# The products with V in an attention loop: the small and the large pair of query blocks in one run, two runs per head in place of four

## The chip, the cores and the metric

The kernel runs on one core of a Trainium2 chip. The metric is the device time of one execution in microseconds (us). It is compared with the kernel before, whose median over 3 runs is 2402.06 us.

## The reference, cut to what matters

Two decoder layers over 1024 tokens of width 1024. Each layer has a mixer (attention with 8 heads beside a causal convolution with 31 taps, then an output projection) and a gated feed-forward part. All is float32, and the large products are done as three products of rounded parts. Only the attention is touched here:

```
for window, dilation in DILATED_PATTERNS:
    o_i, lse_i = _dilated_branch(qp, kp, vp, window, dilation)   # softmax(q k^T * dh**-0.5 + band) v
...
w = jax.nn.softmax(jnp.stack(lses, axis=0), axis=0)
o = jnp.einsum('gbsh,gbshd->bshd', w, jnp.stack(outs, axis=0).astype(jnp.float32))
```

The kernel computes the mixture as one causal softmax: the logarithm of the number of patterns in which a key counts is added to its score (tile logcount), so for a query block of 128 rows all key blocks up to its own are needed.

## The kernel before, in words

The program is written by hand, one instruction queue for each engine, with semaphores between them. What stands in a queue is done in that order; nothing is scheduled by a tool.

Attention of a layer is a loop over steps n = 0 to 75, the same loop in the queues of TensorE (PE), ScalarE (ACT) and VectorE (DVE). There are 64 steps with work of their own: 8 heads times 8 query blocks. Within a head the blocks come in the order BLOCKS = (0, 6, 1, 7, 2, 4, 3, 5); a block b needs b + 1 key blocks. I call the steps of a head its step 0 to step 7. For each of them these things are done, each by its own engine:

- **scores** (PE, `scores`, line 597): q times k, into one of two PSUM tiles mm. It waits until DVE has read that tile two steps before.
- **mask** (DVE, `add_mask`, line 1326): adds logcount, takes the row's maximum, writes the scores to one of four tiles sc. DVE also does some taps of the convolution in these steps (line 1196).
- **exponential** (ACT, `exps`, line 931): in place in sc.
- **turn** (PE, `turn`, line 624), three steps later: transposes the key blocks of sc, up to four into each of three PSUM banks that are used in turn. A bank waits until its last content has been read.
- **copy** (ACT, `read_turn`, line 945): bank to SBUF, into pT_small (it is laid over the tile cos and bears that name in the profile) for steps 0, 2, 4, 6 and into pT_large for steps 1, 3, 5, 7. ACT does in step n of the loop first the copies of step n - 3, and then the exponential of step n.
- **products with V** (PE, `attend`, line 643): two query blocks at a time make a pair. Pair 0 is blocks 0 and 1 (steps 0 and 2) with 3 products, pair 3 is blocks 6 and 7 (steps 1 and 3) with 15, pair 1 is blocks 2 and 3 (steps 4 and 6) with 7, pair 2 is blocks 4 and 5 (steps 5 and 7) with 11. The two blocks of a pair write the two halves of the partitions, so each product uses 64 columns of the array where all other products use 128; the trace has two records for one such product. Before its first product `attend` waits for the copies of its second block, all of them.

After the four pairs ACT moves the head's result out (line 954), PE turns it back four steps later (tile sin, line 624), DVE divides by the row sums (lines 1344 and 1346), and every second head PE turns the finished heads once more (tile rinv), and ACT (line 948) and DVE (line 1336) write x_hi and x_lo. Odd heads from head 3 on have two of these last turns in their steps 1 and 3.

Where the pairs stand is in one table: ATTENDS has for each pair its step in the loop (n = 8 h + that number for head h), the pair and the step that it waits for.

Of the kernel before, what the change touches and what calls it, by code (L numbers as in the profile page):

```python
# [76 lines left out]
O_AT = 25  # L77
H_AT = 15
BLOCKS = (0, 6, 1, 7, 2, 4, 3, 5)
ATTENDS = ((6, 0, 2), (8, 3, 3), (10, 1, 6), (12, 2, 7))  # L80
LAST_STEP = STEPS + 12
DOWN = GROUPS * KT
X_UPD = 2 * KT + DOWN
# [94 lines left out]
def trunk(nc, xT, positions, weights, gains, qk_gains, conv_par, ffn_par, inv_freq, mask, outT):  # L178
    ctx = ExitStack()
    with ctx:  # L180
# [143 lines left out]
        def at(l, per_layer, base, step=0, i=0):  # L324

            return l * per_layer + i * step + base
# [16 lines left out]
        def pT(n):  # L343

            buf, qb = (pT_small, pT_large)[n % 2], BLOCKS[n % TB]
            first = qb if qb % 2 else 0
            return buf[:, first:first + qb + 1, :]
# [20 lines left out]
        def bank_read(l, f, after=0):  # L368

            return at(l, BANK_FILLS[f % TURN_BANKS], f // TURN_BANKS + 1 + after)  # L370

        def plain(eng):


            eng.sem_inc(waits_passed, 1)
# [96 lines left out]
        def _(pe):  # L472
# [15 lines left out]
            for l in range(DEPTH):  # L488
# [80 lines left out]
                def turn_v(t):  # L569

                    pe.wait_ge(mm_read, at(l, MM, U_V + t + 3))
                    if t == 0:
                        pe.wait_ge(small_read, at(l, SMALL, S_LN + 1))
                    else:
                        pe.wait_ge(v_turned, at(l, PAIRS, t))
                    src = v_raw[t]
                    for b in range(TB):
                        last = pe.transpose(stat_s[:, b * P:(b + 1) * P], src[:, b * P:(b + 1) * P], ident[:])  # L578
                    last.then_inc(v_turn_full, 1)
# [6 lines left out]
                def scores(n):  # L586
                    h, qb = n // TB, BLOCKS[n % TB]
                    b = h % 2
                    if n % TB == 0:
                        pe.wait_ge(head_loaded[b], at(l, 80 * HEADS // 2, 80 * (h // 2 + 1)))  # L590
                    pe.wait_ge(mm_read, at(l, MM, M_SCORE + n + 1))

                    keys = (qb // 2 + 1) * 2 * P
                    for a in range(0, keys, BANK):
                        z = min(a + BANK, keys)
                        for k in (k_hh, k_ll):
                            last = pe.matmul(mm[n % 2][:, a:z], q_st[b][:, qb * P:(qb + 1) * P], k[b][:, a:z],  # L597
                                             start=k is k_hh, stop=k is k_ll)
                    last.then_inc(mm_full, 1)

                def turn(f):

                    n, kind, which, a, z = FILLS[f]
                    bank = turn_bank[f % TURN_BANKS]
                    pe.wait_ge(pt_read[f % TURN_BANKS], bank_read(l, f))
                    if f == 2:

                        pe.wait_ge(v_turned, at(l, PAIRS, PAIRS))
                    if kind == "p":
                        if which == 0:  # L610

                            pe.wait_ge(statb_read, at(l, STAT_B, B_MEAN + 1))
                        pe.wait_ge(exp_done, at(l, STEPS, which + 1))
                        blocks = [sc[which % 4][:, kb * P:(kb + 1) * P] for kb in range(a, z)]
                    elif kind == "h":

                        pe.wait_ge(o_moved, at(l, HEADS, which + 1))
                        blocks = [o_turned[which % 2][:, i * P:(i + 1) * P] for i in range(4)]
                    else:

                        pe.wait_ge(o_read, at(l, HEADS, 2 * which + 4))
                        blocks = [o_nat[:, qb, :] for qb in range(a * 4, a * 4 + 4)]
                    for c, block_ in enumerate(blocks):
                        last = pe.transpose(bank[:, c * P:(c + 1) * P], block_, ident[:])  # L624
                    last.then_inc(pt_full, 1)

                def attend(h, k):

                    _, pair, second = ATTENDS[k]
                    b, hh = h // 2, h % 2  # L630
                    if h == 0 and k == 0:
                        pe.wait_ge(v_turned, at(l, PAIRS, PAIRS))
                    if k == 0 and (l or h):

                        pe.wait_ge(o_moved, at(l, HEADS, h))
                    last_fill = LAST_FILL[h * TB + second]
                    for f in range(max(0, last_fill + 1 - TURN_BANKS), last_fill + 1):
                        pe.wait_ge(pt_read[f % TURN_BANKS], bank_read(l, f, 1))
                    cols = slice(pair * P, (pair + 1) * P)
                    for kb in range(2 * pair + 2):  # L640
                        for half in range(2):
                            if kb <= 2 * pair + half:
                                last = pe.matmul(o_bank[half * HEAD_DIM:(half + 1) * HEAD_DIM, cols],  # L643
                                                 vp[b][:, kb, hh * HEAD_DIM:(hh + 1) * HEAD_DIM],
                                                 pT(h * TB + BLOCKS.index(2 * pair + half))[:, kb, :],
                                                 start=kb == 0, stop=kb == 2 * pair + half)
                    last.then_inc(step_done, 1)

                def out_part(u, b, which, k0):

                    pe.wait_ge(weights_split, at(l, UNITS, U_OUT + u + 3))
                    pe.wait_ge(mm_read, at(l, MM, M_OUT + 2 * u + b + 1))
                    for k in which:
                        cols = slice((b * 4 + k) * P, (b * 4 + k + 1) * P)
                        last = split_product(mm[b], (w_hi[u % 2][:, cols], w_lo[u % 2][:, cols]),
                                             (x_hi[:, k0 + k, :], x_lo[:, k0 + k, :]), k == 0, k == 3)
                    if k == 3:
                        last.then_inc(mm_full, 1)

                for n in range(LAST_STEP):  # L660
                    if n == STEPS + 5:
                        pe.wait_ge(o_split, at(l, 2 * PAIRS, 2 * PAIRS - 2))
                        out_part(0, 0, [0], 0)
                    if n == STEPS + 8:
                        out_part(0, 0, [1], 0)
                    if n < STEPS:
                        scores(n)
                    if n == 0:
                        turn_v(3)
                        plain(pe)  # L670
                    attends = [((n - first) // TB, k) for k, (first, _, _) in enumerate(ATTENDS)
                               if (n - first) % TB == 0 and 0 <= n - first < STEPS]
                    for h, k in attends:
                        if k % 2:
                            attend(h, k)
                    for f in range(PT):
                        if FILLS[f][0] == n and FILLS[f][1] == "p":
                            turn(f)
                    for h, k in attends:
                        if k % 2 == 0:  # L680
                            attend(h, k)
                    for f in range(PT):
                        if FILLS[f][0] == n and FILLS[f][1] in "ho":
                            turn(f)
                    if n == LAST_STEP - 1:
                        out_part(0, 0, [2], 0)
# [931 lines left out]
```

## Time and profile before

| | us |
|---|---|
| median of 3 runs (2401.87 to 2402.41) | 2402.06 |
| the profiled execution, its own time | 2402.06 |
| its span in the trace | 2400.3 |
| PE busy, share of the span | 99% |
| ACT busy, share of the span | 33% |
| DVE busy, share of the span | 64% |

The span runs from the first to the last instruction. Busy shares are averages over stages; the attention loop lies, for the first layer, between 250 and 374 us, and for the second between about 1442 and 1566 us. The TensorE clock that was granted is full speed throughout.

### The profile page before, as it was taken

The page shows a single profiled execution, that of the slowest core. Times are in us where ns is not written, and L with a number is a line of the kernel's source. Part 1 is how long each engine was busy: PE and PEld are TensorE (multiplying, and loading weights), DVE is VectorE, ACT ScalarE, POOL GpSimd, SP SyncE. Part 2 cuts the span into 40 slices and gives each one's busy share as a digit, 9 for nine tenths or more (in the row PEclk, how much of TensorE's full clock was granted, in tenths as well). Part 3 has the DMA queues.
Part 4 walks back from the last instruction along what each step waited for, and adds up shares of the span by engine and source line. Part 5 has one row for each costly group of instructions (what it writes and reads, how often), then busy time and mean ns, then how long its engine had stood idle before and what let it go on. Part 6 is the DMA issues. An engine that isn't in the chain of part 4 may idle for free.

```text
span 2400.3 us, 30716 instructions
## 1 busy us (share of the span) xinstructions
PE 2370.7 (99%) x11672; PEld 1945.4 (81%) x11672; DVE 1546.4 (64%) x1659; ACT 788.6 (33%) x1050; POOL 162.0 (7%) x57
## 2 busy tenths in 40 slices
PE   8999999999999999999999999999999999999999
PEld 6888788888888888888788887888888888888887
DVE  5999875656565555555749997755655565555555
ACT  5322675432222222222332227743322222222221
POOL 0122002100000000000102120011000000000000
PEclk9999999999999999999999999999999999999999
DMA  4323631121111111111112254301211111111111
GB/s 159 91 79 111 152 81 36 53 62 52 45 35 52 52 52 44 47 49 44 44 35 80 79 140 116 80 27 53 62 44 53 44 37 50 52 52 44 52 44 70
DMA packets 46676, 153.44 MB, mean 64 GB/s; under 512 B 7424, under 2 KB 10112, under 8 KB 46592
## 3 DMA queue, kind: packets, MB, share of 16 engines
q1 hardware_dynamic: 45728, 149.93, 21.5%
q10 hardware_dynamic: 864, 2.36, 0.2%
q8 instruction: 57, 0.93, 0.2%
q14 instruction: 27, 0.22, 0.0%
HBM read 131.02 MB, written 21.23 MB: 63 GB/s over the span
## 4 chain that ended last, share of the span: by engine, by line
PE 90%; issue 4%; DVE 4%; ACT 1%; DVEq 0%; POOLq 0%; DMA 0%; POOL 0%; SPq 0%; ACTq 0%
PE mm L485 60%; PE aux L485 20%; PE aux L643 3%; PE aux L624 3%; PE mm L597 3%; PE aux L512 1%; DVE y L1196 1%; DVE x_lo L1122 1%; PE aux L521 0%; DMA x<-xT 0%; POOLq L1504 0%; DVE sc L1326 0%; PE aux L578 0%; DVE w_lo L1110 0%; DVE o L1245 0%
## 5 line engine op out<-in xcount | busy, mean ns | idle before, releaser
L485 PE MATMUL mm<-x_hi,w_hi 128*128 128x512 f32 x1920 | 598.7, 393 | 14.3 <-DVE x_lo L1122 11.3
L485 PE MATMUL mm<-x_hi,w_lo 128*128 128x512 f32 x1920 | 594.6, 391 | 0.0
L485 PE MATMUL mm<-x_lo,w_hi 128*128 128x512 f32 x1920 | 594.1, 391 | 0.0
L485 PEld LDWEIGHTS mm<-x_hi,w_hi 128*128 128x128 f32 x1920 | 358.0, 188 | 92.0 <-issue 12.2
L485 PEld LDWEIGHTS mm<-x_lo,w_hi 128*128 128x128 f32 x1920 | 360.7, 188 | 78.3
L485 PEld LDWEIGHTS mm<-x_hi,w_lo 128*128 128x128 f32 x1920 | 360.7, 188 | 77.6
L794 ACT ACTIVATE w_hi<-w_raw 128x1024 fp32r<-128x1024 f32 x152 | 160.0, 1060 | 659.3 <-PE mm L485 461.5
L1116 DVE TENSOR_TENSOR x<-x,aux 128x1024 f32<-128x1024 f32 x176 | 214.8, 1221 | 121.2 <-PE aux L485 111.5
L1110 DVE TENSOR_TENSOR w_lo<-w_raw,w_hi 128x1024 fp32r<-128x1024 f32 x152 | 190.3, 1257 | 54.5 <-ACT w_hi L794 50.7
L1128 DVE TENSOR_TENSOR uv<-mm,rinv 128x1024 f32<-128x1024 f32 x44 | 53.9, 1225 | 220.3 <-PE mm L485 220.1
L1196 DVE SCALAR_TENSOR_TENSOR y<-u_all,cpar,y 128x512 f32<-128x512 f32 x248 | 186.9, 768 | 0.1
L1128 DVE TENSOR_TENSOR ug<-mm,rinv 128x1024 f32<-128x1024 f32 x44 | 53.9, 1225 | 181.2 <-PE mm L485 158.7
L1326 DVE CUSTOM_DVE_ANT_0 sc<-mm,logcount 128x128 f32<-128x128 f32 (+7 forms) x128 | 95.7, 755 | 46.6 <-PE mm L597 26.9
L485 PE MATMUL mm<-x_hi,q_first 128*128 128x512 f32 x384 | 121.4, 397 | 0.0
L485 PE MATMUL mm<-x_lo,q_first 128*128 128x512 f32 x384 | 121.0, 396 | 0.0
L485 PE MATMUL mm<-x_hi,k_hh_first 128*128 128x512 f32 x384 | 120.9, 396 | 0.0
L931 ACT ACTIVATE sc<-sc,small 128x128 f32<-128x128 f32 (+7 forms) x128 | 100.0, 781 | 24.2 <-DVE small L1326 23.2
L1196 DVE SCALAR_TENSOR_TENSOR y<-u_all,taps_sum,y 128x512 f32<-128x512 f32 x120 | 102.7, 855 | 2.6 <-ACT y L850 1.8
L485 PE MATMUL aux<-h_hi_odd,w_hi 128*128 128x512 f32 x320 | 101.0, 397 | 0.0
L485 PE MATMUL aux<-h_lo_odd,w_hi 128*128 128x512 f32 x320 | 100.9, 396 | 0.0
L485 PE MATMUL aux<-h_hi_odd,w_lo 128*128 128x512 f32 x320 | 100.9, 396 | 0.0
L1038 ACT ACTIVATE cg<-cg 128x1024 f32<-128x1024 f32 x44 | 46.7, 1062 | 128.5 <-DVE cg L1444 128.5
(190 smaller groups left out, 3008.0 us busy)
## 6 DMA issues: line engine op xcount, KB each, us to landing
w_raw<-weights SPq DMA_DIRECT2D x188, 512.0 KB, 3.6
qk_scratch<-m SPq DMA_DIRECT2D x64, 128.0 KB, 2.1
qk_scratch<-o SPq DMA_DIRECT2D x64, 128.0 KB, 2.1
x_hi<-qk_scratch SPq DMA_DIRECT2D x32, 256.0 KB, 6.2
q_first<-qk_scratch SPq DMA_DIRECT2D x8, 512.0 KB, 4.6
k_hh_first<-qk_scratch SPq DMA_DIRECT2D x16, 256.0 KB, 5.8
k_ll_first<-qk_scratch SPq DMA_DIRECT2D x16, 256.0 KB, 6.5
x_hi<-qk_scratch SPq DMA_DIRECT2D x8, 512.0 KB, 4.6
```

The lines of the kernel that those rows point to most:

```text
L485: last = pe.matmul(acc[:, cols], a, b[:, cols], start=start and n == 0, stop=stop and n == 2)
L597: last = pe.matmul(mm[n % 2][:, a:z], q_st[b][:, qb * P:(qb + 1) * P], k[b][:, a:z], start=k is k_hh, stop=k is k_ll)
L624: last = pe.transpose(bank[:, c * P:(c + 1) * P], block_, ident[:])
L643: last = pe.matmul(o_bank[half * HEAD_DIM:(half + 1) * HEAD_DIM, cols], vp[b][:, kb, hh * HEAD_DIM:(hh + 1) * HEAD_DIM], pT(h * TB + BLOCK ...
L794: act.activation(w_hi[slot][:], w_raw[raw][:], ACT.Copy).then_inc(w_hi_ready, 1)
L931: act.activation(s, s, ACT.Exp, bias=neg_max[:, n % 4:n % 4 + 1], scale=-1.0, accum_out=row_sum[:, h % 2, qb:qb + 1]).then_inc(exp_done, 1)
L1038: act.activation(cg[:], cg[:], ACT.Silu).then_inc(gate_ready, 1)
L1110: dve.tensor_tensor(w_lo[slot][:], w_raw[base % 2][:], w_hi[slot][:].bitcast(F32), ALU.subtract).then_inc(weights_split, 1)
L1116: dve.tensor_tensor(t, t, buf[:], ALU.add).then_inc(read, 1)
L1128: dve.tensor_tensor(dst, mm[buf][:], rinv[:], ALU.mult).then_inc(mm_read, 1)
L1196: op = dve.scalar_tensor_tensor(y_odd if kind == "odd" else y_even, src[:, i:i + HALF_SEQ], par, y_odd if kind == "odd" and i else y_even, ...
L1326: dve.tensor_tensor_reduce(sc[n % 4][:, 0:keys], mm[n % 2][:, 0:keys], logcount[:, SEQ - keys:SEQ], -SCALE, 3e38, ALU.add, ALU.min, neg_ma ...
```

## The change

Pair 3 is taken to the same step as pair 0, and pair 2 to that of pair 1. All products with V of a step now stand behind the step's scores and ahead of its turns. Nothing else is changed: no instruction is added or removed, on ACT, DVE, POOL and SP the order stays as it was, and the waits of every instruction stay too.

```diff
-ATTENDS = ((6, 0, 2), (8, 3, 3), (10, 1, 6), (12, 2, 7))
+ATTENDS = ((7, 0, 2), (7, 3, 3), (11, 1, 6), (11, 2, 7))
...
                     for h, k in attends:
-                        if k % 2:
-                            attend(h, k)
+                        attend(h, k)
                     for f in range(PT):
                         if FILLS[f][0] == n and FILLS[f][1] == "p":
                             turn(f)
-                    for h, k in attends:
-                        if k % 2 == 0:
-                            attend(h, k)
```

PE's queue around the first run of head 0 (steps 6 to 8 of the loop). sc3 is the tile of step 3, L597 are scores, L624 turns, L643 products with V (`cos` for pair 0, `pT_large` for pair 3), x15 a count of products.

```order
 L624 MATMUL aux0<-ident,sc3 128x128 x4
 L624 MATMUL aux1<-ident,sc3 128x128 x4
-L643 MATMUL aux1<-cos,sa 64x128 x3
 L597 MATMUL mm1<-k_hh_first,q_first 128x512
 L597 MATMUL mm1<-k_ll_first,q_first 128x512
 L597 MATMUL mm1<-k_hh_first,q_first 128x256
 L597 MATMUL mm1<-k_ll_first,q_first 128x256
+L643 MATMUL aux1<-cos,sa 64x128 x3
+L643 MATMUL aux1<-pT_large,sa 64x128 x15
 L624 MATMUL aux0<-ident,sc0 128x128 x3
 L597 MATMUL mm0<-x_hi 128x256 x2
-L643 MATMUL aux1<-pT_large,sa 64x128 x15
```

Pair 0 moves back past the scores of step 7, and pair 3 moves ahead past the turns of step 4 and the scores of the next head's step 0. Between the turns of step 3 (sc3) and the 15 products that need their copies there now stand four score products and three products with V.

PE's queue around the second run of head 0 (steps 10 to 12 of the loop), in the same form; here `cos` is pair 1 and `pT_large` pair 2, and sc3 is the tile of step 7.

```order
 L624 MATMUL aux0<-ident,sc3 128x128 x4
 L624 MATMUL aux1<-ident,sc3 128x128 x2
+L597 MATMUL mm1<-x_hi 128x512 x4
 L643 MATMUL aux1<-cos,sa 64x128 x7
-L597 MATMUL mm1<-x_hi 128x512 x4
+L643 MATMUL aux1<-pT_large,sa 64x128 x11
 L624 MATMUL aux0<-ident,sc0 128x128
 L597 MATMUL mm0<-x_hi 128x512 x2
-L643 MATMUL aux1<-pT_large,sa 64x128 x11
```

The scores of the next head's step 3 now come ahead of pair 1, and pair 2 ahead of the turns of the next head's step 0.

## Rows read from the trace of the kernel before

**Rows 1.** The page's busy times of the engines, with their share of the span.

```profile
PE 2370.7 (99%) x11672; PEld 1945.4 (81%) x11672; DVE 1546.4 (64%) x1659; ACT 788.6 (33%) x1050; POOL 162.0 (7%) x57
```

**Rows 2.** Busy time by stretch: the attention loops of both layers.

```profile
core 0: us, PE busy (x) PEld busy (x) DVE busy (x) ACT busy (x) POOL busy (x), PEclk, DMA share, GB/s
250.00:374.00 124.00, 119.89 (x1080) 100.01 (x1079) 94.98 (x202) 99.50 (x240) 7.15 (x3) 1.00 0.40 95
1465.00:1588.00 123.00, 121.19 (x1038) 100.63 (x1037) 86.42 (x175) 88.61 (x210) 11.36 (x5) 1.00 0.28 65
```

**Rows 3.** The critical chain in the first layer's attention: start, length, what.

```profile
262.69 1.90 PE aux L643 x30
...
370.06 1.90 PE aux L643 x30
...
374.10 2.37 PE aux L643 x36
376.47 1.62 PE mm L485 x6
```

**Rows 4.** Timeline of PE, steps 55 to 63, heads 6 and 7: start, length, what.

```profile
351.03 1.03 PE L624 MATMUL aux<-ident,sc 128*128 128x128 f32 x8
352.00 0.66 PE L643 MATMUL aux<-cos,v_fourth 128*64 128x128 f32 x6
352.58 0.50 PE L597 MATMUL mm<-k_hh_first,q_first 128*128 128x512 f32 x1
...
353.39 0.49 PE L624 MATMUL aux<-ident,sc 128*128 128x128 f32 x3
...
354.07 0.48 PE L597 MATMUL mm<-x_hi 128*128 128x256 f32 x2
354.48 1.97 PE L643 MATMUL aux<-pT_large,v_fourth 128*64 128x128 f32 x30
356.38 0.77 PE L624 MATMUL aux<-ident,sc 128*128 128x128 f32 x5
356.90 1.17 PE L597 MATMUL mm<-x_hi 128*128 128x512 f32 x4
357.91 0.60 PE L624 MATMUL aux<-ident,sc 128*128 128x128 f32 x4
...
359.02 0.82 PE L624 MATMUL aux<-ident,sc 128*128 128x128 f32 x6
359.77 1.09 PE L643 MATMUL aux<-cos,v_fourth 128*64 128x128 f32 x14
360.79 1.20 PE L597 MATMUL mm<-x_hi 128*128 128x512 f32 x4
...
363.03 1.53 PE L643 MATMUL aux<-pT_large,v_fourth 128*64 128x128 f32 x22
364.49 0.98 PE L624 MATMUL aux<-ident,sc 128*128 128x128 f32 x7
...
367.74 0.66 PE L643 MATMUL aux<-cos,v_fourth 128*64 128x128 f32 x6
```

**Rows 5.** Timeline of ACT, steps 57 to 62, with idle time before in brackets.

```profile
359.42 1.04 ACT L931 ACTIVATE sc<-sc,small 128x896 f32<-128x896 f32 x1 [0.28 <-DVE small L1326]
...
360.94 0.86 ACT L945 ACTIVATE pT_large<-aux 128x512 f32<-128x512 f32 x2
...
363.48 1.15 ACT L931 ACTIVATE sc<-sc,small 128x1024 f32<-128x1024 f32 x1 [0.97 <-DVE small L1326]
...
364.62 0.58 ACT L948 ACTIVATE x_hi<-aux 128x512 fp32r<-128x512 f32 x1
...
365.58 0.98 ACT L945 ACTIVATE pT_large<-aux 128x512 f32<-128x512 f32 x2
...
367.29 0.85 ACT L931 ACTIVATE sc<-sc,small 128x640 f32<-128x640 f32 x1
...
368.11 1.11 ACT L945 ACTIVATE pT_large<-aux 128x512 f32<-128x512 f32 x2
```

**Rows 6.** Timeline of DVE: the mask of step 57.

```profile
358.29 1.09 DVE L1326 CUSTOM_DVE_ANT_0 sc<-mm,logcount 128x896 f32<-128x896 f32 x1 [0.72 <-PE mm L597]
```

## The prediction, as it was put on record

> **What bounds the kernel now.** I read the page's busy times first: PE is busy for 99% of the span, the others are far below [rows 1]. Then the busy time of the two attention loops, since the change moves nothing else: PE 119.9 of 124 us and 121.2 of 123, ACT 99.5 and 88.6 [rows 2]. So PE sets the time there too, but ACT has far less room than its 33% over the whole kernel says. The critical chain shows the rhythm: from the first large run (30 records, pair 3 of head 0) at 262.69 to that of head 7 at 370.06 are 107.37 us, 15.3 per head; from there to the first product of the output projection are 6.41 [rows 3]. The profiled execution took 2402.06 us, 1.8 more than its span, and equals the median of the runs, so I add differences to 2402.06.
>
> **What is removed: crossings between 64-column and 128-column products.** Eight turns take 1.03 us and three 0.49, so they follow each other every 0.108 us and one alone takes 0.27. From the start of eight turns to the first product with V are 0.97 us (351.03 to 352.00); seven spacings are 0.76, which leaves 0.21 for the crossing [rows 4]. Between turns and scores it is 0.03 (turns of step 52 and of head 5, 353.39 to 354.07, 0.68 for 7 transposes). So going in from turns costs 0.18 extra. Going in from scores costs about 0.09 extra (354.07 to 354.48 is 0.41, against 0.32 that two such scores take ahead of turns, 1.11 from 357.91 to 359.02 less seven spacings and 0.03). Going out: 14 records take 1.02 until the next scores, 22 take 1.46 until the next turns, and the two together, with no crossing between, 2.37 [rows 3, 4]; a joint is 0.11 cheaper than a crossing. Joining two runs therefore saves 0.18 + 0.11 = 0.29 us, twice per head, 8 heads, 2 layers: 32 x 0.29 = **9.4 us**. That is what PE alone would give.
>
> The Trainium skill says so too (TensorEngine Tiling (Array Packing), Key Properties): changing the tiling mode drains TensorE. The rows agree with 0.18 to 0.21 us at each entry; by that rule alone the time would fall by those 9.4 us, which is my first rival below.
>
> **What is moved, and what it collides with.** The order on ACT stays. In step n it copies the turns of step n - 3 and only then does exponential n. In the new order the 15 and the 11 products stand ahead of the turns whose copy ACT wants next, so ACT stands still during most of a run, and after it has everything to do until the next run, which waits for the last copy of its second block. I walk through one head. X is the start of the 15 products, Y that of the 11; times are row differences.
>
> *From Y to the next X, ACT.* The 11 products take 1.46, one turn 0.27, and 0.05 until ACT sees it (exponential after mask: 359.38 to 359.42 [rows 5, 6]): 1.78. ACT then does: the copy of one block, 0.16 (a copy of four is 0.48, half of 364.62 to 365.58; a block less is 0.11 less, as between the exponentials of 8 and 7 blocks, 1.15 and 1.04); the exponential of step 3, 1.14 (363.48 to 364.62); the move of the result, 0.48; copies and an exponential of steps 1, 2 and 4, 1.71 (365.58 to 367.29); the exponential of step 5, 0.82; the copies of step 3, 1.11 (368.11 on) [rows 5]. Sum 1.78 + 5.42 = 7.20, and 0.1 until PE goes on: **7.3**. With the last turns of an odd head one more copy, 0.48: **7.8**.
>
> *The same, PE.* 1.46 for the products; 2.24 less the 1.01 of four scores, less 0.09, for the single turn and the scores of step 4 (1.14, with four last turns in it; without them and their wait 0.6); 3.25 less 0.18 up to where pair 0 stood (364.49 to 367.74); scores of step 7, 0.81 + 0.09; pair 0, 0.58 less 0.11: 6.5, odd 7.0 [rows 4]. So PE **waits 0.8 us ahead of every large run**. Before, the copies of step 3 (368.11 + 1.11 = 369.22) were done 0.8 us ahead of the large pair at 370.06.
>
> *From X to Y, PE.* 1.90 for the 15 products, 0.68 turns, 0.32 scores, 1.53 turns and scores (356.38 to 357.91), 0.65 turns and scores (357.91 to 359.02 less 0.46 for the odd head's last turns), 0.57 turns of step 7, then the scores of step 3, 1.11, and pair 1, 0.91: 7.67, odd 8.13. One wait is new: those scores need the mask of step 1, two steps before, out of the PSUM tile, and pair 1 no longer stands ahead of them. Scores of step 1 start at 3.42 and end at 4.59, the mask starts 0.22 later (358.07 to 358.29) and takes 1.09: 5.90 [rows 4, 6]; PE is there at 5.65 (odd 6.11). Wait 0.3 in even heads: **8.0**. ACT, from that mask: exponential 1.04, copies of step 7 0.86, latency: 7.9; odd, with one more copy, **8.4** [rows 5]. So in odd heads PE waits there too.
>
> *Sum.* A head takes 8.0 + 7.3 = 15.3, an odd one 8.4 + 7.8 = 16.2. The first of the seven intervals has no result turned back in it, 0.4 less: 14.9 + 3 x 15.3 + 3 x 16.2 = 109.4, against 107.37: +2.0 us per layer.
>
> *The end of the loop.* Before, the large pair of head 7 stood ahead of turns 61; now it is ahead of turns 60, so copy 60, the exponential of step 63 and copies 61 to 63 all come after it. From X: turns 60 done 2.4, copy 2.8, exponential 3.7 (0.93, as for six blocks), copy 61 4.4. Three banks are in turn, so turns 62 wait until DVE has read head 6 (about 4.0), turns 63 until copy 61 (4.5); the last two pairs start at 5.3 and take 2.37: 7.7, against 6.41. **+1.3 us per layer**. Nothing behind this can absorb it: the last head goes from there through ACT, PE and DVE to the output projection.
>
> Total: 2 x (2.0 + 1.3) = +6.6, **2408.7 us**. The wait lengths are the uncertain part: a latency of 0.05 to 0.16 at each of four hand-overs per head moves it by about 2 us each way.
>
> The Trainium skill has a rule that speaks against this change (same page, PSUM Bottleneck): making TensorE faster with tiles does not make the evacuation of PSUM faster, and the copy may become the bottleneck. The walk agrees, with ACT's 7.3 against PE's 6.5; by that rule, taken as ACT setting the pace everywhere, the time is the one above.
>
> **The rivals.**
> 1. *The crossings win*: 2402.06 - 9.4 = 2392.7. For it: PE is 99% busy, its order is all that changes, and copies were done 0.8 us ahead of their run. Against: that is just the lead which is now used up, since ACT starts later by the whole large run. It decides if ACT can be done with its 5.4 us before PE has walked its own part from Y to X, that is, if the chain from Y is below 6.5 instead of 7.3. Chance 0.12.
> 2. *About even*: the waits are there, but ACT's exponentials find other gaps, the wait for the mask does not arise and the end of the loop costs half: 2 x (2.0 - 1.0 + 0.6) = +3, 2405. Chance 0.20.
> 3. *Worse*: turns behind a run also wait for their banks, since copies come late, above all in odd heads, where DVE has to read a bank as well; 0.3 to 0.5 us in each of 16 heads on top, 2415. Against: in the walk each bank is free 0.05 to 0.6 us before it is needed. Chance 0.10.
>
> **How the numbers follow.** My forecast has 0.58; the time is its time. No change that a measurement of this kernel can tell is within 0.2%, 2397.3 to 2406.9. Faster is rival 1, 0.12. Slower is most of the forecast and rival 3; the forecast with short latencies falls just inside the 0.2%, and rival 2 does: same 0.24, slower 0.64. The range leaves out rival 1 and most of rival 3, and takes in rival 2 and the bounds of the latencies: 2400 to 2414.
>
> **What would show it.** Right: PE idle ahead of the L643 runs of 30 records, released by ACT's copies (pT_large, L945), some 0.8 us per head; smaller waits ahead of the scores of step 3 (released by DVE, L1326); ACT idle for more than 1 us ahead of the copy of step 4, released by PE; large runs 15.3 to 16.2 us apart, 109.4 in all; 7.7 us from the last of them to the output projection; entries from turns gone. Wrong: large runs some 14.1 us apart in even heads with no wait ahead of them (rival 1), or waits ahead of turns, released by ACT or DVE (rival 3).

## The result, and the profile after

The changed kernel takes 2417.7 us (median of 4 runs, 2417.32 to 2418.89), the kernel before 2402.11: a ratio of 1.0064, with a 95% interval from 1.0052 to 1.0076. It is slower, as forecast, but by 15.6 us in place of 6.6, and lies outside the range.

The page of the profiled execution (span 2415.5 us) and its busy time in the two attention loops:

```profile
PE 2369.3 (98%) x11672; PEld 1946.2 (81%) x11672; DVE 1547.3 (64%) x1659; ACT 787.5 (33%) x1050; POOL 153.5 (6%) x57
```

```profile
250.00:385.00 135.00, 122.31 (x1121) 103.31 (x1120) 95.38 (x202) 100.65 (x242) 7.13 (x3) 1.00 0.36 87
1457.00:1592.00 135.00, 124.26 (x1122) 104.23 (x1123) 92.51 (x195) 95.17 (x233) 7.12 (x3) 1.00 0.32 75
```

In each line of the second fence the stretch is followed by its length and PE's busy time. PE's busy time over the kernel is 1.4 us less than in [rows 1]. The second stretch of [rows 2] (1465 to 1588) isn't the second loop: it starts 23 us after the loop's first scores and ends 20 us past the loop, and the second stretch here also takes in 8 us ahead of the loop. So I compare the loops from their first scores to the first product of the output projection. They take 134.26 us in the first layer and 134.28 in the second, against 126.65 and 126.63 before: 2 x 7.6 = 15.2 us, all that lies between the two profiled spans (2415.5 and 2400.3). Within them PE is idle for 12.7 us in each layer, against 4.1 before (ACT is busy for 100 us of them in both kernels). The chain that ended last, with the lines that answer to [rows 3]:

```profile
262.39 1.97 PE aux L643 x30
...
359.57 1.97 PE aux L643 x30
...
376.18 1.97 PE aux L643 x30
...
384.02 1.59 PE mm L485 x6
```

The large runs of heads 0 and 7 are 113.79 us apart (before 107.37, forecast 109.4), and from the start of the last to the output projection are 7.76 by the timeline (before 6.41, forecast 7.7). The wait ahead of the large run, in the timelines of ACT and PE in heads 5 and 6 (behind the second run of head 5, whose 11 products start at 352.19):

```profile
352.19 1.53 PE L643 MATMUL aux<-pT_large,v_third 128*64 128x128 f32 x22
...
354.01 0.28 ACT L941 ACTIVATE cos<-aux 128x128 f32<-128x128 f32 x1 [1.48 <-PE aux L624]
354.19 1.14 ACT L927 ACTIVATE sc<-sc,small 128x1024 f32<-128x1024 f32 x1
355.32 0.59 ACT L950 ACTIVATE sin<-aux 128x512 f32<-128x512 f32 x1
355.80 0.98 ACT L941 ACTIVATE pT_large<-aux 128x512 f32<-128x512 f32 x2
...
357.51 0.85 ACT L927 ACTIVATE sc<-sc,small 128x640 f32<-128x640 f32 x1
358.32 1.10 ACT L941 ACTIVATE pT_large<-aux 128x512 f32<-128x512 f32 x2
...
359.57 1.97 PE L643 MATMUL aux<-pT_large,v_fourth 128*64 128x128 f32 x30 [0.75 <-ACT pT_large L941]
```

ACT stands idle for 1.48 us while PE does the 11 products and the turn behind them, then works without a gap, and PE waits 0.75 us for the end of its last copy. From Y (352.19) to X (359.57) are 7.38 us, 7.3 in the walk. The smaller wait that the prediction named is there too, ahead of the scores of step 3 in even heads, 0.3 us as in the walk:

```profile
350.17 0.50 PE L597 MATMUL mm<-k_hh_first,q_first 128*128 128x512 f32 x1 [0.29 <-DVE small L1322]
```

What the walk had not: VectorE. Its timeline, and ACT's and PE's where they wait for it, behind the large run of head 4:

```profile
327.23 0.51 PE L643 MATMUL aux<-pT_large,v_third 128*64 128x128 f32 x5 [0.75 <-ACT pT_large L941]
...
330.14 0.20 DVE L1340 RECIPROCAL small<-small 128x8 f32<-128x8 f32 x1 [2.03 <-PE aux L624]
330.43 0.69 DVE L1342 TENSOR_TENSOR rinv<-aux,small 128x512 f32<-128x512 f32 x1
...
331.44 0.29 DVE L1322 CUSTOM_DVE_ANT_0 sc<-mm,logcount 128x128 f32<-128x128 f32 x1 [0.32 <-issue]
331.65 0.75 DVE L1192 SCALAR_TENSOR_TENSOR y<-u_all,cpar,y 128x512 f32<-128x512 f32 x1
...
332.32 1.08 DVE L1322 CUSTOM_DVE_ANT_0 sc<-mm,logcount 128x896 f32<-128x896 f32 x1
...
333.44 1.05 ACT L927 ACTIVATE sc<-sc,small 128x896 f32<-128x896 f32 x1 [0.56 <-DVE small L1322]
```

The head's result is turned back behind the large run, so the division by the row sums (L1340, L1342) waits 2.03 us for it, and masks 0 and 1 of the next head stand behind it in VectorE's queue. It starts at X + 2.91 (330.14 less 327.23). In the kernel before it had no wait and started at X + 0.84 (X is 354.48 there, [rows 4]):

```profile
355.32 0.19 DVE L1344 RECIPROCAL small<-small 128x8 f32<-128x8 f32 x1
```

Mask 1 ends at X + 6.17 (333.40 less 327.23); my walk had 5.90.

And in the steps of head 3, the first in which last turns of finished heads come (GpSimd is POOL):

```profile
298.97 2.38 POOL L1516 TENSOR_TENSOR u_all<-u_all,y 128x1024 f32<-128x1024 f32 x1 [28.00 <-DVE y L1192]
299.82 2.09 DVE L1192 SCALAR_TENSOR_TENSOR y<-u_all,cpar,y 128x512 f32<-128x512 f32 x1
...
301.84 0.41 DVE L1322 CUSTOM_DVE_ANT_0 sc<-mm,logcount 128x256 f32<-128x256 f32 x1
302.18 0.74 DVE L1192 SCALAR_TENSOR_TENSOR y<-u_all,cpar,y 128x512 f32<-128x512 f32 x1
...
302.84 0.68 DVE L1332 TENSOR_TENSOR x_lo<-aux,x_hi 128x512 fp32r<-128x512 f32 x1
...
303.62 1.53 PE L643 MATMUL aux<-pT_large,sb_ 128*64 128x128 f32 x22 [1.45 <-DVEq L1334]
```

A tap that takes 0.75 us otherwise takes 2.09 beside GpSimd's sum of 2.38. The mask, another tap and the read of x_lo stand behind it, and the 11 products, whose wait takes in the bank that x_lo is read from, start after 1.45 us of idle time. In heads 3, 5 and 7 PE also waits for VectorE ahead of the turns of step 2 (0.69, 0.69 and 0.40 us at 308.46, 340.81 and 372.86); the kernel before has no wait there.

### The profile page after: what moved, and what is told of

Its sections match the earlier page's. It is cut to its first block, busy times and chain, and to the rows that moved or that the text cites. A ratio compares the mean times of both kernels' runs of the same rounds, so it can differ in the third digit from the quotient of the medians.

```text
span 2415.5 us, 30716 instructions
## 1 busy us (share of the span) xinstructions
PE 2369.3 (98%) x11672; PEld 1946.2 (81%) x11672; DVE 1547.3 (64%) x1659; ACT 787.5 (33%) x1050; POOL 153.5 (6%) x57
## 4 chain that ended last, share of the span: by engine, by line
PE 87%; issue 5%; DVE 4%; ACT 2%; POOLq 0%; DVEq 0%; DMA 0%; POOL 0%; ACTq 0%; SPq 0%
PE mm L485 60%; PE aux L485 20%; PE aux L643 3%; PE aux L624 2%; PE mm L597 1%; DVE y L1192 1%; PE aux L512 1%; ACT pT_large L941 1%; ACT sc L927 1%; DVE sc L1322 1%; PE aux L521 0%; POOLq L1500 0%; DVE x_lo L1118 0%; DVE w_lo L1106 0%; PE aux L578 0%
## 5 line engine op out<-in xcount | busy, mean ns | idle before, releaser
L485 PE MATMUL mm<-x_hi,w_hi 128*128 128x512 f32 x1920 | 599.1, 393 | 14.2 <-DVE x_lo L1118 11.3
L1112 DVE TENSOR_TENSOR x<-x,aux 128x1024 f32<-128x1024 f32 x176 | 214.9, 1221 | 121.2 <-PE aux L485 111.5
L624 PE MATMUL aux<-ident,sc 128*128 128x128 f32 x576 | 86.0, 277 | 5.9 <-DVEq L1334 3.6
```

Source lines behind the costliest of these rows:

```text
L485: last = pe.matmul(acc[:, cols], a, b[:, cols], start=start and n == 0, stop=stop and n == 2)
L1112: dve.tensor_tensor(t, t, buf[:], ALU.add).then_inc(read, 1)
```

## The experiments

The stretches that the runs are compared by: X is the start of the 30 records of pair 3, Y that of the 22 of pair 2, from the traces' start times. Even are the stretches in the steps of heads 4 and 6, odd those in the steps of head 5. Both layers agree within 0.03 us there. The kernel before had medians of 2402.1 to 2402.4 beside these runs. X and Y are starts of products, not fixed places in PE's queue: where a run stands one step earlier or later, another share of the work lies between them, so X to Y and Y to X compare only kernels with the same places, and head to head compares all. The profiled executions of some kernels are 1 to 2 us above their median; their first loop then starts that much later (at 252.0 us for 249.7 in the last one), and the stretches inside the loops are not touched by it.

| kernel | median us | X to Y even, odd | Y to X even, odd | head to head, even, odd | last X to output |
|---|---|---|---|---|---|
| before | 2402.1 | 7.59, 8.55 | 7.13, 7.20 | 14.72, 15.75 | 6.41 |
| changed | 2417.7 | 8.25, 8.74 | 7.39, 7.96 | 15.64, 16.70 | 7.76 |
| first run only | 2410.4 | 8.59, 9.82 | 6.37, 6.27 | 14.95, 16.10 | 7.76 |
| second run only | 2408.2 | 6.99, 7.47 | 8.08, 9.04 | 15.06, 16.51 | 6.41 |
| exponential first | 2414.1 | 8.26, 8.75 | 6.86, 7.96 | 15.12, 16.71 | 7.76 |
| tap moved | 2416.7 | 7.99, 8.47 | 7.39, 7.96 | 15.38, 16.43 | 7.76 |
| bank not waited for | 2416.1 | 8.25, 8.74 | 7.38, 7.96 | 15.63, 16.70 | 7.76 |
| GpSimd's sums late | 2413.5 | 8.25, 8.74 | 7.38, 7.96 | 15.63, 16.70 | 7.76 |
| all four | 2406.9 | 7.99, 8.46 | 6.86, 7.96 | 14.85, 16.42 | 7.76 |
| before, sums late | 2399.2 | 7.59, 8.55 | 7.13, 7.19 | 14.72, 15.74 | 6.41 |
| last head as before | 2416.1 | 8.25, 8.74 | 7.38, 7.96 | 15.63, 16.70 | 6.41 |
| one join at pair 3's place | 2400.2 | 7.65, 8.62 | 6.99, 6.95 | 14.64, 15.56 | 6.47 |
| both joins there | 2405.4 | 7.55, 9.44 | 6.96, 7.04 | 14.50, 16.48 | 6.47 |
| one join there, sums late | 2397.7 | 7.65, 8.62 | 6.99, 6.95 | 14.64, 15.56 | 6.47 |
| and the second in heads 0, 1, 3, 5 | 2396.5 | 7.55, 8.62 | 6.96, 6.95 | 14.50, 15.56 | 6.47 |

**One half of the change alone.** Two kernels join only one of the two runs; the other pairs keep their old place. Shown is the edit against the kernel before; the comments are mine, and `...` stands for what is left out.

```diff
-ATTENDS = ((6, 0, 2), (8, 3, 3), (10, 1, 6), (12, 2, 7))
+ATTENDS = ((7, 0, 2), (7, 3, 3), (10, 1, 6), (12, 2, 7))   # first run only
...
-                        if k % 2:
+                        if k != 2:                          # pair 1 stays behind the turns
                             attend(h, k)
...
-ATTENDS = ((6, 0, 2), (8, 3, 3), (10, 1, 6), (12, 2, 7))
+ATTENDS = ((6, 0, 2), (8, 3, 3), (11, 1, 6), (11, 2, 7))   # second run only
...
-                        if k % 2:
+                        if k != 0:                          # pair 0 stays behind the turns
                             attend(h, k)
```

> Only pairs 0 and 3 are joined (both in step 7); pairs 1 and 2 stand where they stood before. Theory A (ScalarE's queue: its copies and exponentials are shut out during the large run and must then be done before the next one): pair 2 still stands ahead of the next turns as before, so ScalarE catches up there only in part; waits ahead of the 15 products of 0.3 to 0.6 us, and the end of the loop costs 1.3 us per layer as in the changed kernel, since pair 3 of the last head stands ahead of the last turns there too: about 2407 us. Theory B (the loss comes from the second run alone, whose wait takes in the bank that VectorE reads, and whose scores wait for a mask): 2402.1 - 16 x 0.29 = 2397.5 us.

> Only pairs 1 and 2 are joined (both in step 11); pairs 0 and 3 stand where they stood before. Theory A: ScalarE has a whole microsecond more before the next 15 products, so no wait there; the wait for the mask ahead of the scores of step 3 (0.3 to 0.5 us in even heads) and that for the bank which VectorE reads (1.2 us in head 3, 0.3 in heads 5 and 7) remain, and 16 x 0.29 = 4.6 us of crossings are saved: 2401 to 2404 us, no loss at the end of the loop. Theory B: nearly the whole loss of the changed kernel, 2417.7 + 4.6 = 2422 us at most, 2412 at least.

2410.4 us (ratio 1.0032, interval 1.0020 to 1.0045) and 2408.2 us (1.0024, 1.0014 to 1.0034). Against 2402.4 beside them, each half costs, 8.0 and 5.7 us where the whole costs 15.6: theory B falls, and both numbers of theory A were too low, by 3 and by 4 us or more. In the first, the waits ahead of the 15 products are 0.28 to 0.36 us from head 2 on, as theory A had them, but a turn in head 3 waits 1.36 us for VectorE's bank (0.29 before), and that head takes 17.3 us for 16.1. In the second, the turns of step 2 of heads 3, 5 and 7 wait 0.7, 0.7 and 0.4 us for VectorE's bank, as in the changed kernel, and even there ACT is late, not for pair 3, but for pair 0, for which I had expected nothing:

```profile
356.48 0.66 PE L643 MATMUL aux<-cos,v_fourth 128*64 128x128 f32 x6 [0.25 <-ACT cos L945]
```

The first half has the whole of the 1.35 us at the end of the loop, the second none, as expected.

**ScalarE's order.** Only in the steps with a run the exponential goes ahead of the copies, so ACT has it to do during the run.

```diff
+                    ahead = n >= 7 and n % TB in (3, 7)
+                    if n < STEPS and ahead:
+                        exps(n)
                     for f in range(PT):
                         if FILLS[f][0] == n and FILLS[f][1] == "p":
                             read_turn(f)
-                    if n < STEPS:
+                    if n < STEPS and not ahead:
                         exps(n)
```

> The changed kernel, but ScalarE does in the two steps with a run (steps 7 and 3 of a head) the exponential ahead of the copies, so it has 0.93 and 1.15 us of work while TensorE does the large products. Theory A: the wait ahead of the 15 products disappears (from the second run's large part to the next first one 6.5 to 6.6 us in even heads instead of 7.39), the wait for the mask and VectorE's bank stay; in all about 5 us per layer less than the changed kernel: 2407 to 2409 us. Rival (the waits come from the transposes' banks or from TensorE's long runs themselves): no change, 2417 to 2418 us.

2414.1 us (1.0048, 1.0032 to 1.0065), 3.6 less, of the 9 to 11 expected: the size was missed. In even heads Y to X falls from 7.39 to 6.86: the mechanism is there. In odd heads it stays at 7.96. The timelines of VectorE, ACT and PE of this kernel in head 5 tell why:

```profile
335.42 1.22 DVE L1325 CUSTOM_DVE_ANT_0 sc<-mm,logcount 128x1024 f32<-128x1024 f32 x1 [0.32 <-issue]
336.69 1.15 ACT L927 ACTIVATE sc<-sc,small 128x1024 f32<-128x1024 f32 x1 [1.06 <-DVE small L1325]
...
338.00 0.59 ACT L944 ACTIVATE x_hi<-aux 128x512 fp32r<-128x512 f32 x1
...
339.35 0.68 DVE L1335 TENSOR_TENSOR x_lo<-aux,x_hi 128x512 fp32r<-128x512 f32 x1
...
340.13 0.44 PE L624 MATMUL aux<-ident,sc 128*128 128x128 f32 x2 [0.69 <-DVEq L1337]
```

The mask of step 3 stands behind VectorE's first x_lo and starts only at 335.42; so the exponential that was to fill the run waits 1.06 us for it, and then x_hi, x_lo and the turns of step 2 wait in a row. In odd heads ACT and VectorE hold each other up, by this timeline, and ACT's order changes nothing; no run takes the two apart there.

**VectorE's tap.**

```diff
-TAPS_AT = (1, 1, 1, 0, 1, 1, 1, 1)
+TAPS_AT = (0, 1, 1, 1, 1, 1, 1, 1)
```

> The changed kernel, but VectorE does no tap of the convolution in step 0 of a head and one in step 3 instead. Theory: in the changed kernel the result of the last head is turned back 1.9 us later, VectorE's division by the row sums waits for it, and masks 0 and 1 of the next head stand behind it, so mask 1 ends 0.25 us later than in my walk; without the tap between them mask 1 starts about 0.28 us earlier: the stretch from the 15 to the 11 products shortens from 8.25 to 8.0 us in even heads, 1.5 us in all: 2416.2 us. Rival (ScalarE alone sets that stretch): no change, 8.25 us.

X to Y is 7.99 in even heads for 8.25, as expected: the mask is what the division and the tap behind it hold up. Odd heads gain the same 0.27. The total says little: the two executions took 2415.95 and 2417.45 us (ratio 1.0058, interval 1.0038 to 1.0078), which takes in both the 2416.2 expected and no change. The first X comes 1.0 and 0.7 us later after the start of the loop, and head 3, where a tap of 2.74 us now meets GpSimd's sum, takes 18.2 us in the second layer for 17.9. In the first layer of the profiled execution, the slower of the two, it takes 19.9, with 2.50 us for 22 records that take 1.53 otherwise, and I know no cause.

**The bank in the wait.** The last three banks before a run are waited for, and in odd heads one of them is VectorE's, which the products do not need.

```diff
                     for f in range(max(0, last_fill + 1 - TURN_BANKS), last_fill + 1):
+                        if FILLS[f][1] == "o":
+                            continue
                         pe.wait_ge(pt_read[f % TURN_BANKS], bank_read(l, f, 1))
```

> The changed kernel, but the products with V do not wait for the bank that VectorE reads (the last turn of the finished heads), which they do not need. Theory (in odd heads the second run waits for VectorE behind a mask and a tap): the 11 products start 1.2 us earlier in head 3 and 0.2 to 0.3 earlier in heads 5 and 7; a part comes back, since the mask of step 3 still stands behind VectorE's read: 1 to 3 us less in all, 2415 to 2416.7 us. Rival (that wait is only one that ends last beside ScalarE's copies): under 0.5 us, 2417.5 us.

One of its two executions took 11.7 ms, with PE busy about five times as long as otherwise; the other took 2416.4 us. I know no cause and read nothing from it. The same kernel once more:

> The kernel of the run before in which one execution took 11.7 ms, once more, since that one told nothing. The same expectation: the 11 products of head 3 start 1.2 us earlier, those of heads 5 and 7 0.2 to 0.3, part of it comes back behind them; 2415 to 2416.7 us. Rival: 2417.5 us.

2416.1 us (2 runs; 1.0057, 1.0039 to 1.0076). The 11 products of head 3 come 1.16 us earlier (X to Y 8.73 for 9.89), and 0.55 of that is given back up to the next X (8.51 for 7.96), as expected. In heads 5 and 7 nothing moves, against the 0.2 to 0.3 expected: there ACT's copy ended at the same time, and the longer 8.74 comes from the late mask, as the run with the tap moved shows (8.47).

**GpSimd's sums.** They go behind the last tap, in the changed kernel and in the one before.

```diff
-                    pool.wait_ge(tap_done, at(l, N_TAPS, TAP_LAST[c] + 1))
+                    pool.wait_ge(tap_done, at(l, N_TAPS, TAP_LAST[CT - 1] + 1))
```

> The changed kernel, but GpSimd makes its three sums of the convolution's results only behind the last tap, so none of them runs beside the taps in heads 0 and 3. Theory (the taps of 2.7 and 2.1 us there, beside GpSimd's sums of 2.4 us, hold up the masks): the stretch behind the second run of head 0 falls from 8.16 to 7.4 us and the one of head 3 from 9.89 to 8.9: 1.7 us per layer, 3.4 in all, 2414.3 us. Rival (the long taps are hidden): no change, 2417.7 us.

> The kernel before with GpSimd's three sums behind the last tap. Its intervals show 1.15 us more behind the second large pair of head 0 (8.28 against 7.13) and 0.42 in head 3 (8.97 against 8.55) than in the others: without them 2402.1 - 2 x 1.57 = 2399.0 us. Then of the 4.2 us that the same edit gave in the changed kernel only about 1.1 belong to the change. Rival (those stretches are longer for another reason): 2402.1 us.

2413.5 us (1.0046, 1.0030 to 1.0062) and 2399.2 us (0.9986, 0.9976 to 0.9995): near the 2414.3 and 2399.0 expected. In the changed kernel Y to X of head 0 falls from 8.16 to 7.38 and X to Y of head 3 from 9.89 to 8.73. But 3.1 of these 4.2 us the kernel before could gain as well (8.28 to 7.11, and 8.97 to 8.55).

**All four together.**

> The changed kernel with all four edits at once: exponential first in the steps with a run, no wait for VectorE's bank, the tap moved out of step 0, GpSimd's sums late. If these four causes are what the change costs, even heads take 8.0 + 6.9 = 14.9 us and odd ones 8.4 + 7.6 to 8.0, the end of the loop keeps its 1.35 us per layer (there the bank that VectorE reads decides): about 2404.7 us, 2403 to 2407. Rival (a further cause): 2410 us or more.

2406.9 us (1.0021, 1.0012 to 1.0030), at the upper edge. Against the kernel before with the same edit to the sums it is still 7.7 us slower: 2.7 behind the last X, 1.3 ahead of the first, and most of the rest in odd heads (16.42 against 15.74). VectorE's two reads of last turns stand between masks there; that they are the reason is argued, not shown.

**The end of the loop.** The changed kernel, with the last head's pairs in their old places (its pairs 0 and 1 behind the turns again, which is left out here).

```diff
...
+attends = [(h, k) for h in range(HEADS) for k in range(4)
+           if n == h * TB + ((6, 8, 10, 12) if h == HEADS - 1 else (7, 7, 11, 11))[k]]
...
```

> The changed kernel, but the four pairs of the last head of each layer stand where they stood before the change. Theory (at the end of the loop the large run shuts ScalarE and VectorE out, and nothing behind it takes that up): from the 15 products to the output projection 6.41 us again instead of 7.76, and ScalarE's copies are done when the 15 products come; less two joints of 0.29: 0.8 to 1.4 us per layer less than the changed kernel, 2415 to 2416.1 us. Rival (the end is longer only because the wait of 0.9 us ahead of the last 15 products moved behind them): under 0.3 us per layer, 2417.3 us.

2416.1 us (1.0056, 1.0041 to 1.0072). From the last X it is 6.41 again; the interval ahead grows by 0.63, so 0.75 us per layer are a loss of the end itself, the low end of what I expected, and 0.6 were moved.

**A run where the next turn stands ahead of it.** Pair 0 goes to pair 3's old place, not the other way round, and pair 1 to pair 2's in the second kernel. The first is an edit of the kernel before, the second of the changed one; the comments are mine.

```diff
-ATTENDS = ((6, 0, 2), (8, 3, 3), (10, 1, 6), (12, 2, 7))
+ATTENDS = ((8, 0, 2), (8, 3, 3), (10, 1, 6), (12, 2, 7))   # one join
...
-                        if k % 2:
+                        if k != 2:                          # pair 1 stays behind the turns
                             attend(h, k)
...
-ATTENDS = ((7, 0, 2), (7, 3, 3), (11, 1, 6), (11, 2, 7))
+ATTENDS = ((8, 0, 2), (8, 3, 3), (12, 1, 6), (12, 2, 7))   # both joins
```

> The kernel before, but pair 0 is joined to pair 3 where pair 3 stood (step 0 of the next head, behind the turns of step 4, ahead of those of step 5); pairs 1 and 2 stand apart as before. ScalarE then has the copy of step 4 and the exponential of step 7 to do while the 15 products run. Theory (a run costs nothing when the next turn stands ahead of it): the crossing is saved, 0.29 us per head; 0.15 of it is lost where the result's transposes now wait for the bank of step 3's first copy: 16 x 0.14 to 16 x 0.29 less than before, 2397.5 to 2400 us. Rival (a joint gives nothing by itself, the crossings' price is hidden elsewhere): 2402 us or more.

> As the changed kernel, two joined runs per head, but each one step later, where the large pair stood, behind the turns of step 4 and of the next head's step 0. Theory: first run as in the kernel with that join alone (0.14 to 0.29 us saved per head); the second saves 0.29 in even heads less 0.3 for the mask that the scores of step 3 wait for, and loses 0.2 to 0.6 in odd heads, where the turn of step 0 waits for VectorE's bank with pair 1 no longer ahead of it: 2399 to 2403 us, in any case over 12 us below the changed kernel. Rival (joined runs are slow wherever they stand): 2412 us or more.

2400.2 us (0.999, 0.998 to 1.000), just above the range, and 2405.4 us (1.0013, 1.0004 to 1.0023). The first total is at the edge of what these runs can tell, but its loops are shorter by 1.05 and 1.03 us. It shows both sides of the matter. ACT and PE in head 5 of it:

```profile
339.33 0.66 PE L624 MATMUL aux<-ident,sin 128*128 128x128 f32 x4
...
340.64 1.92 PE L643 MATMUL aux<-pT_large,v_third 128*64 128x128 f32 x28
340.91 0.49 ACT L945 ACTIVATE cos<-aux 128x384 f32<-128x384 f32 x1 [0.44 <-PE aux L643]
341.30 0.93 ACT L931 ACTIVATE sc<-sc,small 128x768 f32<-128x768 f32 x1
```

The turns of step 4 are done ahead of the run, and ACT does their copy and the exponential of step 7 while PE does the 15 products. An even head gains 0.08 us. The joint's 0.29 is lessened by the wait of the result's transposes for their bank (339.33, 0.22 us after the start of the last turn for 0.11, and their first takes 0.33 for 0.27: 0.17 in all), which I had put at 0.15; a further 0.04 isn't explained. The second kernel is 2.4 us above the upper end of its range: even heads are the fastest so far, 14.50, but odd ones take 16.48, 0.9 more than in the first kernel, where I had put the loss at 0.2 to 0.6. PE's timeline in one of them:

```profile
333.09 0.33 PE L624 MATMUL aux<-ident,sc 128*128 128x128 f32 x1 [1.11 <-DVEq L1334]
```

The turn of step 0 waits for VectorE's bank, with pair 1 no longer ahead of it.

From these, two kernels that keep only what paid:

> The kernel with one join at the large pair's place, and GpSimd's sums late: 2400.2 less 2 x 1.3 us (8.20 to 6.99 in head 0, 8.75 to 8.62 in head 3) = 2397.5 us, below both kernels. Rival: the sums, now beside the end of the loop, hold up VectorE there: 2400 us.

> The kernel with one join at the large pair's place and GpSimd's sums late (2397.7 us), and the second join too (pairs 1 and 2 where pair 2 stood), but only where no last turns of finished heads stand in those steps: heads 0, 1, 3 and 5. Theory: even intervals were 14.50 us with both joins and 14.64 with one, so 4 x 0.14 per layer, 1.1 us in all: 2396.6 us. Rival (the two joins add nothing, the mask takes it): 2397.7 us.

2397.7 us (0.9979, 0.9970 to 0.9988) and 2396.5 us (0.9976, 0.9967 to 0.9985), both as expected. The last beats both kernels, by 5.6 us against before; about 3 of them come from GpSimd's sums, and the joints are worth 2.7 (2399.2 less 2396.5, and each loop takes 123.76 us for the 125.1 of the kernel before with the sums late). What its even heads still wait for, in the timeline of PE's weight loads:

```profile
344.47 0.19 PEld L597 LDWEIGHTS mm<-k_hh_first,q_first 128*128 128x128 f32 x1 [0.27 <-DVE small L1326]
...
352.74 0.42 PEld L624 LDWEIGHTS aux<-ident,sin 128*128 128x128 f32 x4 [0.19 <-ACT pT_large L945]
```

The scores of step 3 wait for the mask and the result's transposes for their bank.

## Why the prediction was right in sign and wrong in size

The waits were forecast in kind, and the range was missed for two reasons: the walk from X to Y left out VectorE's queue, and the walk of a quiet head was compared with a measured sum that isn't quiet.

**The crossings** (9.4 us). Compatible with the price of 0.29, which no run isolates: 14.72 less two joints would be 14.14 us for an even head, and the last kernel has 14.50 with the two waits just shown in it, without which it would be 14.0 to 14.2 (an estimate from these rows). That PE's busy time fell by 1.4 us only does not speak against it: behind a wait a record no longer overlaps the one before (0.27 us long at a spacing of 0.108 in [rows 4]), so part of the saving comes back as busy time. But 0.22 of 0.58 is all that an even head keeps even at the best place found; the rest goes into waits that the crossings had covered.

**From Y to X** (7.3 and 7.8). Right in size: 7.39 and 7.96, with the wait ahead of X released by ACT's copies as described (they end at 359.42, and the products start 0.15 us later for the 0.1 of the walk). In odd heads the wait for VectorE's bank ahead of the turns of step 2 (0.69 us), which the walk did not have, also lies in this stretch, so that ACT alone sets it there is not shown. That ScalarE's shut-out is the cause in even heads is shown by putting the exponential first (6.86) and by putting the run behind the turn (6.96).

**From X to Y** (8.0 and 8.4). The step that failed. The walk took the mask of step 1 as starting 0.22 us after its scores, with VectorE free. It starts 0.5 us after them (332.32, scores done by 331.81), since the division by the row sums now waits for the result's transposes, which the change puts behind the large run, and it and a tap stand ahead of that mask: 8.25 and 8.74. The tap moved out of the way gives 7.99 and 8.47, the numbers of the walk. In head 3 it came to 9.89, by GpSimd's sum, a tap of 2.09 us and the wait for VectorE's bank, none of which I had in the walk. I had named the division only at the end of the loop.

**The sum.** +2.0 us per layer between the runs was measured as +6.4 (113.79 less 107.37). By stretches, measured less forecast: 0.9 in head 0 behind the second run (8.16 for 7.3) and 1.5 in head 3 come from head 7's rows being taken for all heads; 0.75 and 0.7 are the late mask in even and odd heads; 0.3 and 0.4 are latencies from Y to X: 4.5. The first of these is an error of method: I added up a walk through a quiet head and compared it with a measured sum that has 1.57 us per layer of GpSimd's contention in it, 3.1 us in all. Of the 15.6 us the contention itself explains little, since the change costs 14.3 (2413.5 less 2399.2) without it. Compared with the quiet kernel before, whose runs are 105.83 us apart, the same walk gives 2 x (109.4 - 105.83 + 1.3) = 9.7 us in place of 6.6. The other 4.6 are the late mask in all heads (2 x 1.8) and the latencies (2 x 0.67), less the first X, which comes 0.16 us earlier than before.

**The end of the loop** (1.3). Right in length, 7.76 us; what it costs by itself is 0.75 us per layer, the rest is a wait moved.

**The rivals.** That crossings win is refuted, and so is that it comes out about even. The third, turns that wait for banks held too long, had the nearest size (2415), and its sign is there in the odd heads from head 3 on, where turns wait 0.4 to 0.7 us for a bank that VectorE reads. In the other heads no new wait of this kind shows, and that the size came near is in part luck: more of the miss comes from the late mask and the comparison of the sums.

**[rows 2].** Its second stretch isn't the second loop. From 1442 to 1566 us PE is busy for 119.88 and ACT for 99.61 us, so the two layers are alike, and no term of the sum used the 121.2 and 88.6.

What stays open: with all four causes relieved, 7.7 us remain. They lie, by the intervals, in odd heads, at the end and ahead of the first run, and I tried no kernel that moves the last turns of finished heads.

## What to carry to other kernels

Before joining two runs on the engine that sets the pace, look at which in-order queue has its next piece of work behind the run: put the run behind the instruction that feeds that queue, not ahead of it, and the same joint turned here from a loss of 8.0 us into a gain of 2.2 (1.5 with GpSimd's sums late in both kernels). A walk must go through every queue that stands between the events, also those that were never late before, and be compared with a walk of the kernel before by the same method, not with its measured sum.

## What I had not expected of the hardware

A tap on VectorE, 0.75 us long, took 2.09 us beside a GpSimd sum of 1024 columns that itself took 2.38, and the kernel before gained 3.1 us when the sums were moved away from the taps. The tap of 2.09 us ended 0.56 us after the sum did (301.91 and 301.35), and one of 2.74 us in head 0 of the same execution 0.55 us after its sum (271.53 and 270.98); the sums take 2.38 us beside a tap and, in the kernel before with the sums late, 2.38 to 2.40 without one. It looks as if the tap hardly moves until the sum is done. What the two engines share there was not tested. And one execution of one kernel took 11.7 ms in place of 2.4: PE was busy for 11692 us in place of some 2370, with records 3.7 to 3.8 times as long (the products of line 485 took 1496 ns for 393 in the mean), at a granted clock of 1.0, while VectorE and ACT were busy for as long as usual (1534.5 and 802.2 us). A second run of the same program was normal, and nothing here tells the cause.
